# SyncE's loads in a head step reordered, and one late pair's column sums moved three tiles on

## The reference

```
m = silu(cond) @ w_ada + b_ada          # six rows of 2048 for each of two conditions: shift, scale, gate, twice
h = rmsnorm(x) * (1 + scale) + shift
z = h @ w_in                            # q, k, v of 12 heads of 128, and 512 SSM channels
attn = softmax(q k / sqrt(128) + relative position bias, context keys beside) v
ssm  = bidirectional complex scans in 32 groups, then GLU
x = x + gate1 * (concat(attn, ssm) @ w_out)
x = x + gate2 * experts(rmsnorm(x) * (1 + scale2) + shift2)   # 16 experts, each takes its best tokens
```

## Time and profile before

| | |
|---|---|
| median of 3 runs | 2378.49 us (2372.06 to 2381.67) |
| profiled execution | 2373.38 us, span 2371.6 us |
| busy PE, DVE, ACT, POOL | 2212.6, 757.9, 622.1, 645.6 us |
| mean granted PE clock | 0.983 |
| bytes | 625.74 MB, mean 264 GB/s |

### The profile page before, as it was taken

The page is one execution under the profiler, slowest core; times in us unless marked ns, Lnnn a source line. Parts: engine busy times, 40 slices in busy tenths (PEclk is TensorE's granted clock), DMA queues, the critical chain, the costliest instruction groups (busy, mean ns, idle before and its releaser), DMA issues.

```text
span 2371.6 us, 58683 instructions
## 1 busy us (share of the span) xinstructions
PE 2212.6 (93%) x25709; PEld 1513.6 (64%) x25709; DVE 757.9 (32%) x1260; ACT 622.1 (26%) x1436; POOL 645.6 (27%) x662
## 2 busy tenths in 40 slices
PE   5999999999999999998997689999999999999997
PEld 3468888767667667543443666667666666666674
DVE  4124444366666767356524100000000000000001
ACT  3011111244444444335445121111111111111100
POOL 0236772355545545057720100000000000000000
PEclk9999999999999999999998899999999999999999
DMA  9932322344444443677754989999999999999996
GB/s 370 371 89 55 93 55 81 114 127 131 124 135 129 119 139 107 266 254 223 229 179 162 337 321 404 408 410 408 409 409 414 416 413 410 407 408 382 407 415 227
DMA packets 188383, 625.74 MB, mean 264 GB/s; under 512 B 18862, under 2 KB 95448, under 8 KB 158444
## 3 DMA queue, kind: packets, MB, share of 16 engines
q1 hardware_dynamic: 153496, 552.82, 60.9%
q10 hardware_dynamic: 31220, 48.30, 6.3%
q0 software_dynamic: 3424, 20.97, 3.4%
HBM read 597.59 MB, written 24.44 MB: 262 GB/s over the span
## 4 chain that ended last, share of the span: by engine, by line
PE 69%; DMA 16%; DVE 5%; issue 3%; SPq 2%; ACT 1%; ACTq 1%; POOL 0%; another core or an unknown queue 0%; DVEq 0%; POOLq 0%
PE PS L1974 19%; PE PS L1988 10%; PE PS L1631 10%; PE PS L1772 8%; PE PS L1453 8%; DMA hT_<-in_w_gate 5%; DMA work<-in_w_gate 4%; DMA work<-in_w_ada 3%; PE PS L1330 3%; PE PS L1395 3%; DMA work<-in_w_down 2%; PE PS L1625 1%; SPq L668 1%; PE PS L1357 1%; DMA work<-in_w_in 1%
## 5 line engine op out<-in xcount | busy, mean ns | idle before, releaser
L1974 PEld LDWEIGHTS PS<-hT_,work 128*64 128x64 f32 x14336 | 511.4, 140 | 91.6 <-issue 82.0
L1974 PE MATMUL PS<-hT_,work 128*64 128x80 f32 x14336 | 530.8, 235 | 35.3 <-issue 23.0
L2740 POOL TENSOR_TENSOR work<-work 128x512 f32<-128x512 f32 x240 | 318.8, 1328 | 274.6 <-ACT work L1094 264.0
L1988 PE MATMUL PS<-work,hT_ 128*32 128x512 f32 (+1 forms) x2544 | 304.7, 600 | 7.6 <-DMA work<-in_w_down 4.7
L1772 PE MATMUL PS<-work,mixT_ 128*128 128x512 f32 x640 | 286.6, 602 | 1.9 <-DMA work<-in_w_out 1.9
L2595 DVE TENSOR_TENSOR hT_<-PS,hT_ 128x480 f32<-128x480 f32 x16 | 10.5, 658 | 850.6 <-ACT hT_ L1308 850.6
L1299 ACT ACTIVATE hT_<-PS,small 128x64 f32<-128x64 f32 x248 | 102.3, 413 | 681.7 <-PE PS L1330 681.7
L1631 PE MATMUL PS<-hT_,work 128*128 128x320 f32 x768 | 226.7, 442 | 13.7 <-DMA work<-in_w_in 13.7
L2808 POOL DMA_INDIRECT out_y<-mixT_,work x15 | 22.0, 1466 | 789.8 <-DVE mixT_ L2622 789.8
L1453 PE MATMUL PS<-work,hT_ 128*128 128x256 f32 x960 | 214.2, 382 | 1.7 <-DMA work<-in_w_in 1.7
L1772 PEld LDWEIGHTS PS<-work,mixT_ 128*128 128x128 f32 x640 | 120.1, 192 | 147.4 <-issue 145.2
(11 more groups left out here) (318 smaller groups left out, 2158.9 us busy)
## 6 DMA issues: line engine op xcount, KB each, us to landing
work<-in_w_up SPq DMA_DIRECT2D x57, 2048.0 KB, 23.4
work<-in_w_down SPq DMA_DIRECT2D x56, 2048.0 KB, 33.8
work<-in_w_gate SPq DMA_DIRECT2D x55, 2048.0 KB, 29.7
work<-in_w_in SPq DMA_DIRECT2D x80, 512.0 KB, 5.1
work<-in_w_ada SPq DMA_DIRECT2D x148, 256.0 KB, 2.8
work<-in_w_ada SPq DMA_DIRECT2D x16, 2048.0 KB, 19.3
work<-in_w_ada ACTq DMA_DIRECT2D x108, 256.0 KB, 3.1
hT_<-in_w_gate SPq DMA_DIRECT2D x9, 2048.0 KB
```

The costliest lines, as they stand in the source:

```text
L1974: last = pe.matmul(hidden_at(u, f)[64 * h:64 * h + 64, :], w[:, k % 4, f // 2, f % 2, 64 * h:64 * h + 64], xsT[s][:, k, :], start=opens, s ...
L1988: last = pe.matmul(bank(3 + c)[32 * g:32 * g + n, :], actT[s][:, k, first:first + n], w[:, k % 2, col * BANK:(col + 1) * BANK], start=(k = ...
L2740: TT_(acc_ctx[p % 3], acc_ctx[p % 3], prod[i % 2], ALU.add).then_inc(s_padd, 1)
```

## The change

On SP, for every head h: the last two late loads of a head's twelve are issued in the next head's part, behind the two weight blocks that stood behind them; the cache loads follow these, and the span loads of odd heads are no longer in one piece of 16 behind the late loads but four and four behind the late loads 7 to 10. In the output projection, `late_sums(5)` moves on PE from behind tile (1, 0) to behind tile (1, 3), the row's add on DVE and its store on ACT from (1, 1) to (1, 3), and the load of the seventh pair's bias on ACT from behind tile (1, 3) into the late steps ahead of block n = 2.

```diff
-            def head_spans(i):
-                if i:
+            def head_spans(i, quarters=range(4)):
+                if i and 0 in quarters:
                     sp.wait_ge(s_biasm, 2 * i)
-                for qc in range(16):
+                for qc in range(4 * quarters[0], 4 * quarters[-1] + 4):
...
             for h in range(HEADS):
                 first = LATE_STEP * h + 3
+                pair = (h + 1) // 2 if h % 2 and h + 1 < HEADS else None
                 if h:
                     for n in (4 * h + 3, 4 * h + 4):
                         if RAW <= n < 4 * HEADS:
                             head_block(n)
+                    for m in range(first - 2, first):
+                        late(m)
+                    if h > 1:
+                        head_cache(h)
                 if h - 1 in LATE_SUMS:
                     late_bias(LATE_SUMS[h - 1] + 1)
                 for m in range(first, first + 4):
                     late(m)
                 if h + 1 < HEADS:
                     head_block(4 * h + 5)
-                for m in range(first + 4, first + 8):
-                    late(m)
+                for quarter in range(4):
+                    late(first + 4 + quarter)
+                    if pair is not None:
+                        head_spans(pair, range(quarter, quarter + 1))
                 if h + 1 < HEADS:
                     head_block(4 * h + 6)
-                for m in range(first + 8, first + 12):
+                for m in range(first + 8, first + 10):
                     if m < LATE_HEADS:
                         late(m)
-                if h % 2 and h + 1 < HEADS:
-                    head_spans((h + 1) // 2)
-                if 1 <= h < HEADS - 1:
-                    head_cache(h + 1)
...
                 elif n == 2:
-                    late_steps(214, 22)
+                    late_steps(214, 11)
+                    late_bias(6)
+                    late_steps(225, 11)
                 for tt in range(TT):
                     late_steps(*late_tile(n, tt))
                     square(n, tt)
-                    if (n, tt) == (1, 1):
+                    if (n, tt) == (1, 3):
                         late_pair_out(5)
-                    elif (n, tt) == (1, 3):
-                        late_bias(6)
...
                     last.then_inc(s_omm, 1)
-                    if tt == 0:
+                    if (n, tt) in ((1, 3), (2, 0)):
                         late_sums(4 + n, 7)
...
                     gain(n, tt)
-                    if (n, tt) == (1, 1):
+                    if (n, tt) == (1, 3):
                         late_row_added(5, 7)
```

## The result

| | before | after | ratio, 95% interval |
|---|---|---|---|
| median, first comparison | 2378.10 us (4 runs) | 2355.28 us (4 runs, 2354.16 to 2356.30) | 0.9907, 0.9885 to 0.9928 |
| median, second comparison | 2379.43 us (11 runs) | 2356.40 us (6 runs, 2349.09 to 2363.37) | 0.9904, 0.9885 to 0.9924 |
| profiled execution, its span | 2373.38 us, 2371.6 us | 2354.16 us, 2352.4 us | |
| mean granted PE clock | 0.983 | 0.983 | |

2356 us was forecast. Lines 1330 to 2751 of the kernel before are three higher in the one after (L1631 is L1634, L1708 is L1711, L1718 is L1721, L2390 is L2393); SP's lines up to L676 are the same.

A forecast was written before the change was run, and what follows sets the result against it. PE was taken to set the end. Heads 18.97 us plus moved sums 3 make 22 off the profiled 2373.4, so 2351.4; the median, 5.1 above, gives 2356.5, stated as 2356, range 2344 to 2368.

The forecast's parts named there:

- Rival A: Whole kernel as forecast: heads -19, output projection -3 (0 to -6), 2353 to 2359 us, chance 0.50.
- Heads: Attention heads, five even steps: the spans cost 18.97 us, waits plus slow matmuls behind them, and all of it goes.
- blocks first: Heads, step edges: blocks go out 9.5 us earlier against waits of 2.5 us; all five PE waits go, 18.97 us.
- The late load: Heads, step edges: each step's second late load queues behind two 512 KB blocks; nothing taken, thinnest cover of the change.
- Upper bound 836.9: Heads, edge of steps 8 and 9: latest landing of the second late load behind the blocks, 0.7 us inside the limit.
- 837.6: Heads, same edge: latest late-load start before PE notices; each us beyond costs ten steps one us each.
- 2.6 us for an unhindered one: Heads: time from a late load's issue at 832.23 to VectorE's start at 834.79 with nothing in its way.
- The lower bound, no change: Heads: earliest landing of the second late load behind the blocks, 834.8, as before the change.
- Quarters: Heads: span loads four and four behind late loads +7 to +10, 1.36 us each time, were to cost nothing.
- The sums: Output projection: sixth pair's sums three tiles on; wait worth 11.82 us, 3 taken as gain, bounds 0 and 12.
- halved in rate rather than kept behind all of it: Output projection: ScalarE's late loads, on another queue row than SyncE's 2 MB load, keep half their rate; gain stays 3.
- if it loses 3 us, nothing is left: Output projection: if the stream of late rows loses 3 us to the earlier expert load, the sums' gain is nothing.

The follow-up runs named there:

- q1: Kernel before with only the span loads moved, in quarters behind late loads; late loads and cache stay ahead of the blocks: 2351.26 us, ratio 0.9901.
- d1b: As q1, but only eight of the sixteen span loads moved, eight left ahead of the blocks: 2356.44 us, ratio 0.9909 to the kernel before.
- b1: Kernel before with only the heads' new order, but the 16 span loads whole between weight blocks and late loads: 2372.92 us, ratio 0.9989.
- s1: Kernel before with only the sixth late pair's sums moved, heads as before: 2376.40 us, ratio 1.0012.
- p1: Changed kernel with SyncE's next expert load held until 253 of 256 late steps are done: 2350.19 us, ratio 0.9881 to the kernel before.
- af2: The changed kernel measured once more, no further edit: 2356.40 us, ratio 0.9904 to the kernel before.

## Why the prediction was right, and where it was not

**The time, by its own sum.** 22 us were forecast off the median, and the ratio 0.9907 is 22.1 us. The profiled execution was to be 2351.4 and was 2354.16. Rival A's mechanism happened in the heads; in the output projection it ended at A's lower bound of nothing, or just under it.

**Heads.** 18.97 us were taken for the spans in five even steps: 18.70 measured. That waiting is not the whole cost, and that only some of the waits have slow matmuls behind them, was right too: 13.1 us of idle time and 5.6 of slow matmuls. What the prediction did not settle is which edit is worth it. It gave the gain to "blocks first"; q1 and d1b show that it is the place of the spans, and that going out 2.7 us earlier is enough for a 2.5 us wait. Moving the late loads behind the blocks bought nothing and cost cover.

**The late load.** Upper bound 836.9, "0.7 inside" 837.6. Measured 2.35 us later than before, on before's scale 834.79 + 2.35 = 837.14: just past the bound, 0.5 inside the limit. The load's own condition was met when it was expected: it is issued 0.8 us ahead of the step in both kernels. The "2.6 us for an unhindered one" was read from the start of a row of two issues; from the end of the second it is 1.4. The lower bound, no change, did not hold: the load takes 3.7 us from issue to use behind two blocks and 1.4 without. In the Trainium skill, "DMA: Bandwidth & Descriptors" ("Queues, rings and completion order") has each DMA engine take a queue row's descriptors in ring order, and this trace agrees. The limit itself was measured by b1.

**Quarters.** Forecast nothing, and nothing is seen: no new wait of PE takes the place of the old ones. Steps 1 to 11 gave 22.0 instead of 19.0, by 1.4 in the odd steps (with step 3) and 1.9 in step 11, where eight matmuls behind a load of w_out ran in 3.70 us instead of 5.40. Only the second has a cause in the rows.

**The sums, the term that failed.** The step that failed was "with the stream where it is, PE waits 6.1 us at 1196.1 ... 3.3 us are left". PE's arrival was right (in s1 1196.17). The stream was not where it was: it ended 4.4 us later in the changed kernel, so the wait was 10.3, and with the slow matmuls behind it a little more than nothing was lost: 0.2 - 2.0 = -1.8 us. The prediction had named the reason and left it out of the value: the next expert load goes out 11.4 us earlier (217.29 after the start of step 12, before 228.72), here with eight late adds still to come, and ACT then waits 5.06 us for a late load. p1 shows it, since holding that one load gives 4.6 us back, and so do the last eight adds: 17.0 us with the load among them and 11.7 without. The prediction also had the late loads "halved in rate rather than kept behind all of it". The trace shows less than half: one seventh of the bytes over 4 us, and 7.0 us for one late load instead of 3.2. So the stated condition "if it loses 3 us, nothing is left" was what happened. s1 gives the price by time: +2.8 us (0.5 to 5.2 by its interval).

**Why the sum still held.** Against the forecast the profiled execution has 3.0 us more from the heads, 4.8 less from the output projection, 2.1 less ahead of the heads and 1.1 more behind: 22 - 2.8 = 19.2. The medians differ by more than the two profiled executions do (22.8 in the first comparison), so that these 2.8 us are within what runs differ by, and so are the two small terms. The middle of the range was met because one term came out larger and another smaller, not because each was right.

**Open.** Why the odd steps 5, 7 and 9 lose 0.35 us each: in d1b and b1 they take 125.17 and 125.86, so they lose it only where no piece of the spans is left at the even steps' edge, but no row names the wait. Why the stream of late rows came to its last eight adds at times that differ by some us from trace to trace (217.48 in s1, 224.03 in af2, from the start of step 12) was not followed. What the clock fell for is open too: before, it fell behind waits of 2.54, 2.59 and 3.38 us and stayed up behind 2.47 and 2.72.

## What to carry to other kernels

Before reordering a queue, find the one transfer that is late and what is ahead of it, and move just that, just far enough: here eight small loads taken away gave nearly what a new order of everything gave. When a wait for a slower stream is moved, the stream's end and not the place of the wait sets the time; and whatever PE's progress releases (here a 2 MB load) now starts earlier too and can slow that stream, so hold it or move the consumer. Price idle time of PE with the slow matmuls behind it, here about 1.4 to 1.5 us for each us idle, as a mean over five waits: behind some of them the clock stayed up and nothing was added.

## What was not expected of the hardware

- In b1 the late load of step 2 is issued 5.0 us later than in the changed kernel and is used only 3.2 us later. Right behind two 512 KB blocks it takes 3.5 us from issue to use (527.33 - 523.84); with the blocks out of the way 1.7 (531.08 - 529.36).
- The price of short idle times: 13.7 us in five pieces cost 18.7 us, and 13.2 us in b1 cost 20.4. Waits of about the same length did or did not bring slow matmuls: 2.54 and 2.59 us did, 2.72 did not.
- A 2 MB load issued by SP with eight 256 KB steps to go made those eight take 17.0 us instead of 11.7. It took 9.5 us to landing, and beside it ACT's small packets got one seventh of the bytes.
